# Three reorderings in a decoder trunk: DVE's second level update, GpSimd's fourth level mask, TensorE's first RWKV solution

## The reference, cut to what matters

```
def mixing_block(h, w_in, ...):
    proj = h @ w_in
    u_s5, p_ml, p_rw, p_mb = split_cols(proj, (GW, ML_COLS, RW_COLS, MB_COLS))
    y_s5 = s5_mixer(u_s5, ...)        # diagonal complex scan over time
    y_ml = mlstm_mixer(p_ml, ...)     # qk = silu(causal_dwconv(q, k)); weighted attention
    y_rw = rwkv7_mixer(p_rw, ...)     # delta-rule recurrence over time
    y_mb = moba_mixer(p_mb, rel_bias) # softmax attention with relative bias
    ...
def cross_attention(h, mem_n, wq, wkv, wo):
    kv = (mem_n @ wkv)...             # independent of the mixer
```

## Time and profile before

| | us |
|---|---|
| median of 3 runs | 511.85 |
| the runs | 802.19, 511.85, 511.84 |
| profiled execution | 511.39 |
| its span, first to last instruction | 509.6 |

### The profile page before, as it was taken

How to read it: one execution, slowest core, us unless ns; L and a number is a source line. 1 busy time by engine, 2 the same in 40 slices (tenths; PEclk the granted TensorE clock), 3 DMA queues, 4 the chain that set the end, 5 groups by cost and what they waited for, 6 DMA issues and landing times.

```text
span 509.6 us, 8527 instructions
## 1 busy us (share of the span) xinstructions
PE 489.8 (96%) x3498; PEld 447.1 (88%) x3498; DVE 389.1 (76%) x469; ACT 258.6 (51%) x413; POOL 170.1 (33%) x101
## 2 busy tenths in 40 slices
PE   6999989979899999999999999999999999999995
PEld 4999688969698879888999889999999999988884
DVE  4899989997777987779656457699999999962124
ACT  6678574412432235667855657544454444443432
POOL 0004408487969260000000000253334433454460
PEclk9999999999999999999999999999999999999998
DMA  7976237012122022626555260274455555545502
GB/s 261 367 273 214 84 115 298 11 75 84 57 109 66 19 84 84 247 84 247 182 191 185 105 248 1 91 282 166 166 180 197 202 173 192 203 154 197 213 28 83
DMA packets 12691, 79.19 MB, mean 155 GB/s; under 512 B 1483, under 2 KB 2156, under 8 KB 4076
## 3 DMA queue, kind: packets, MB, share of 16 engines
q1 hardware_dynamic: 12652, 78.65, 43.0%
HBM read 76.80 MB, written 1.84 MB: 154 GB/s over the span
## 4 chain that ended last, share of the span: by engine, by line
PE 76%; DVE 16%; ACT 3%; issue 3%; DMA 1%; DVEq 0%; SPq 0%; ACTq 0%
PE bank L392 75%; DVE we_rest L373 3%; DVE vx L1766 1%; DVE arena L1739 1%; ACT we_high L367 1%; DVE arena L1610 1%; DMA kx<-x_t 1%; DVE bank L1557 1%; DVE wm_rest L373 1%; DVE arena L1731 1%; DVE arena L1732 1%; DVE arena L1762 1%; DVE arena L1751 0%; DVE wk_rest L373 0%; DVE arena L1625 0%
## 5 line engine op out<-in xcount | busy, mean ns | idle before, releaser
L373 POOL TENSOR_TENSOR w_rest<-ring,w_high 128x1024 fp32r<-128x1024 f32 x20 | 48.5, 2422 | 197.4 <-ACT w_high L367 197.4
L392 PE MATMUL bank<-h_high,w_high 128*128 128x256 f32 x384 | 102.9, 283 | 0.0
L367 ACT ACTIVATE w_high<-ring 128x1024 fp32r<-128x1024 f32 x64 | 67.3, 1058 | 69.3 <-PE bank L392 69.2
L392 PE MATMUL bank<-h_rest,w_high 128*128 128x256 f32 x352 | 99.6, 283 | 0.0
L392 PE MATMUL bank<-h_high,w_rest 128*128 128x256 f32 x320 | 90.6, 283 | 0.0
L392 PEld LDWEIGHTS bank<-h_high,w_high 128*128 128x128 f32 x384 | 71.7, 192 | 0.5 <-issue 0.4
L373 DVE TENSOR_TENSOR w_rest<-ring,w_high 128x1024 fp32r<-128x1024 f32 x38 | 48.5, 1282 | 30.0 <-ACT w_high L367 29.9
L392 PEld LDWEIGHTS bank<-h_rest,w_high 128*128 128x128 f32 x352 | 67.6, 192 | 0.0
L392 PE MATMUL bank<-arena 128*128 128x128 f32 (+7 forms) x496 | 58.8, 296 | 4.9 <-DVE arena L1762 2.8
L392 PEld LDWEIGHTS bank<-arena 128*128 128x128 f32 (+3 forms) x496 | 51.6, 178 | 11.8 <-DVE arena L1762 4.4
L392 PEld LDWEIGHTS bank<-h_high,w_rest 128*128 128x128 f32 x320 | 61.4, 192 | 0.0
(11 more groups left out here) (343 smaller groups left out, 1262.3 us busy)
## 6 DMA issues: line engine op xcount, KB each, us to landing
ring<-weights SPq DMA_DIRECT2D x49, 1024.0 KB, 5.0
third_slot<-weights SPq DMA_DIRECT2D x15, 1024.0 KB, 4.9
gain<-gains SPq DMA_DIRECT2D x3, 512.0 KB, 6.1
cst<-consts SPq DMA_DIRECT2D x1, 1472.0 KB, 8.1
par<-params SPq DMA_DIRECT2D x1, 1168.0 KB, 11.7
kx<-x_t SPq DMA_DIRECT2D x2, 512.0 KB, 5.3
ring<-weights SPq DMA_DIRECT2D x2, 512.0 KB, 6.2
vx<-mem_t SPq DMA_DIRECT2D x1, 1024.0 KB, 11.0
```

The source lines that it names most:

```text
L367: nc.scalar.activation(split_half(i)[0], raw_half(i), ACT.Copy).then_inc(S["w_high"], 1)
L373: e.tensor_tensor(rest_, raw_half(i), high.bitcast(F32), ALU.subtract).then_inc(rest_done(i)[0], 1)
L392: return nc.tensor.matmul(out_, lhsT, rhs, start=start, stop=stop, skip_group_check=True)
```

## The change: three moves

No instruction is added, removed or resized. On DVE the projection of `mb_k` and level 2's update go ahead of the rest of half 22, and the silu goes behind the rest of half 23. On POOL `level_mask(4)` goes ahead of `rotate_back(1)`. On PE the first half of `wkv(3)` goes ahead of `solve_u(0)`.

```
@@ PE
             mb_scores(3, 5)
+            wkv(3, 1, (0,))
             solve_u(0, 4)
-            wkv(3, 1, (0,))
             o = pe_open(pe, "S0", 4)
@@ POOL
             rotate(1)
+            level_mask(4)
             rotate_back(1)
-            level_mask(4)
             rotate(2)
@@ DVE
+            project_scaled("mb_k", mqk[:, 2:4, :])
+            level_update(2)
+            rests(H_MID + 6)
             dve.wait_ge(S["ml_silu"], 1)
             ex = v3(E_[:, 0:1024], T)
             v.scalar_tensor_tensor(cv, ex, 1.0, cv, ALU.add, ALU.mult).then_inc(S["ml_qk"], 1)
 
-            rests(H_MID + 5)
-            level_update(2)
-            rests(H_MID + 6)
-            project_scaled("mb_k", mqk[:, 2:4, :])
             moved(dve, "g_col")
```

More of the change, by code:

```diff
@@ L1792, in _ @@
             v.scalar_tensor_tensor(cv, ex, 1.0, cv, ALU.add, ALU.mult).then_inc(S["ml_qk"], 1)
[L1794 to L1797, removed]
             moved(dve, "g_col")
```

## The result

The changed kernel takes 514.43 us as a median of 6 executions (512.86 to 515.19), before 511.85 as a median of 6 taken with them. The ratio is 1.0045, interval [1.0032, 1.0058]: slower by a little under half a percent, clear of the noise between executions, and inside the 2% that the forecast called no change. Forecast were 513.1 and a range of 510.6 to 514.5. The time lies inside the range by only 0.07 us, and three of the six executions lie above it.

The account below looks back on a forecast made before the run. PE, busy 489.8 of 509.6 us, was taken to bound the kernel. From 511.39, minus 0.5 (DVE and POOL moves) plus 1.75 (PE move) gave 512.65 profiled, about 513.1 as a median; range 510.6 to 514.5.

Parts of the forecast that it names:

- Part 1, DVE: Level 2's update on DVE starts 1.67 us earlier, so PE comes out of `level_p(3, ...)` 1.67 us ahead.
- Part 2, POOL: `level_mask(4)` stretches `scan(1)`; the turn back ends at 133.5 instead of 129.40, and `s5_out(1)` on PE waits for it.
- the two engines take turns: DVE and POOL instructions reading two operands from SBUF take turns; masks and scans from 121.85 need 4.5 us together.
- The net of both parts: DVE and POOL moves up to `wkv(0)`: 0.5 us gained of the 2.6 freed; bounds 2.6 and -0.3.
- Part 3, PE: First half of `wkv(3)` ahead of `solve_u(0)` delays DVE's queue; `wkv(4)` starts at 193.95 instead of 192.19, costing 1.75 us.
- S5's argument and the second of POOL's multiplications collide: L1913 on DVE, asked for at 189.05, takes turns with POOL's multiplications; half 32's rest starts at 192.75 instead of 190.82.
- the slower rival: Late turn back makes PE wait for half 25's rest or `level_mask(5)`: up to 1.3 us more, 514.4; chance 0.10.
- parts 1 and 2 are gained in full: Rival: turns cost less, `rotate_back(1)` ends by 131, PE keeps all 2.6 us: 511.0 in total; chance 0.12.
- part 3 is free: Rival: DVE wins every turn against L1080, half 32's rest ends about 192.05: 511.2 in total; chance 0.15.

Follow-up runs that it names:

- the late `h_rest`: Changed kernel with DVE's two reductions ahead of `solution(0)` and its two `h_rest` instructions behind the first two decay weights: 514.08 us, ratio 1.0045 against before.
- the pair alone: Kernel before with the DVE and POOL moves, PE as before: 511.62 us, ratio 0.9989 against before.
- the reductions ahead of the copy: Kernel before with only the PE move, and DVE's two reductions put ahead of `solution(0)`: 511.93 us, ratio 1.0000 against before.
- the filled kernel: Changed kernel plus idle matmuls of constants, eight ahead of `s5_out(1)` and seven ahead of `wkv(4)`, results unused: 512.62 us, ratio 1.0013 against before.
- all three with reductions first: Changed kernel (DVE, POOL and PE moves) with DVE's two reductions ahead of `solution(0)`: 511.04 us, ratio 0.9975 against before.

## Why the prediction was right, and what it missed

*Part 1, DVE.* The update started at 111.50 and `level_p(3, 0)` at 112.81 (forecast 111.6 and 112.9). Right.

*Part 2, POOL.* The turn back was to end near 133.5 and ended at 133.60. That it fits so closely is in part luck. The end of `rotate(1)` was kept at 121.85 and came at 122.41, since L1034 took 5.11 us; masks and scan together were then a little quicker than counted (4.25 us from 122.35 against 4.5), and the turn back took 6.92 against 7.2 (the recorded sum has 2.2 for 2 x 1.15). That the two engines take turns is right: it is shown by the DVE move alone, the POOL move alone, and the late `h_rest`: the four instructions take 5.0, 5.95 or 6.9 us with none, one or two of `h_rest` in them. The net of both parts was forecast at 0.5 us; the pair alone gave 0.2 in the median and 0.35 in the lowest executions. In the changed kernel's profiled execution it was a loss of 0.54: `wkv(0)` started 0.89 us later than in the pair's trace, at the lower clock behind the same wait.

*Part 3, PE.* A new wait of 0.6 us ahead of S0 (0.56) and one ahead of `wkv(4)`, which starts 1.78 us later, counted from `wkv(0)`, where 1.75 was forecast. One detail was incomplete. The trace ends that wait with ScalarE's evacuation of `wkv(3)` (193.81 + 0.58 = 194.39), which shares the bank; the rest of half 32 ends at 194.37. Both hang on S5's argument (L1916), so it is one chain with two ends, and the reductions ahead of the copy free both. That S5's argument and the second of POOL's multiplications collide was right too: L1914 took 2.00 us instead of 0.43. But L1914 is a `tensor_scalar` with one operand from SBUF, so turns are not only for instructions that read two, as the prediction had it.

*The sum.* Forecast +1.25 us, measured +2.6 in the median, twice as much. It still falls into the range, by 0.07 us, and that is luck: the upper bound came from the slower rival, whose mechanism did not occur. The step that was too small is the one that followed the waits only to their ends: "PE would be there at 191.83, and now waits until 193.95". It priced PE's idle time at its length. What lay behind a wait of 2 us at the lower clock cost another 1.5 us at `wkv(4)` and 0.9 at `wkv(0)` in the profiled execution; the prediction has no term for the clock. With PE kept busy the same kernel comes out at 512.62, which is the forecast's sum to half a microsecond (before plus 0.7, against plus 1.25).

*The rivals.* That parts 1 and 2 are gained in full, and that part 3 is free, are refuted by the moves of DVE and POOL together and by the PE move alone. The slower rival named the wrong mechanism: neither half 25's rest nor level 5's mask became a wait.

What stays open: why one execution is granted the lower clock behind such a wait and another is not, why the clock also fell near 120 us in three traces (the PE move alone, with and without the reductions first, and the filled kernel), and whether the other four slower executions of the filled kernel lost theirs there too, since one was traced. The shares of the two filled places were not measured one by one.

## What to carry to other kernels

Before moving an instruction ahead of a short matmul whose result another engine copies, list what is queued behind that copy: here two reductions, eight exponentials, a gelu and a weight's rest were two microseconds late for a wait of 0.9. A gap of an engine that shares a port is not free if its partner is the reason for the gap; count both engines' work on the port from the last fixed point to the next. And count a wait of the matmul engine of about two microseconds as longer than it is, since here work behind it ran at half clock in part of the executions.

## What the runs showed of the hardware that was not expected

TensorE's clock fell from 2.4 to 1.2 GHz for some 3.3 us behind waits of 1.88, 2.14, 3.54 and 3.64 us, while behind one of 2.13 us, in two traces (the DVE and POOL moves, and all three with reductions first), it did not. In the trace of the filled kernel it fell at 117.6 us with no wait above 0.95 us in the 9 us ahead. So a wait of about 2 us is neither enough for the lower clock nor needed for it. The Trainium skill, page "TensorE: Matmul & The Clock Gate", section "Part 1: The HAM clock gate (the "warmup" mystery)", says that recent activity of the engine decides between the two levels; the filled waits agree with that (granted clock from 134 to 138 us 1.00 instead of 0.59, from 194 to 198 us 1.00 instead of 0.67). The fall at 117.6 us is not explained by any run here.

DVE can keep the port over several instructions. In the changed kernel one POOL instruction that began at 113.42, ahead of three DVE instructions of 128x1024 in a row (113.89, 115.02, 116.16), took 5.11 us instead of 1.29, while elsewhere (rows of `h_rest` above) the two alternate. What decides between the two was not tried.
